# The two residual products of a two-layer block, cut by half of the features and 512 columns instead of by 256 columns

## The reference, cut to what matters

```python
# first layer: two mixed branches, back to the residual
x = x + jnp.einsum('bsd,de->bse', merged, w_out[layer])
# second layer: 16 learned meta tokens ahead of the 1024
h = jnp.concatenate([meta, x], axis=1)
u = rmsnorm(h, norm_mix_w);  proj = u @ w_in
h = h + jnp.concatenate([o_gla, o_swa], axis=-1) @ w_out
f = rmsnorm(h, norm_ff_w)
return h + jnp.square(jax.nn.relu(f @ w_ff1)) @ w_ff2
```

## Time and profile before

| | |
|---|---|
| median of 3 runs | 2725.63 us |
| profiled execution | 2722.03 us |
| its span (first to last instruction) | 2720.5 us |
| mean granted TensorE clock | 0.978 of full speed |
| VectorE, ScalarE, GpSimd busy | 61%, 40%, 8% |
| moved by DMA | 278.54 MB, 102 GB/s over the span |

### The profile page before, as it was taken

One profiled execution on the slowest core, in us unless ns is written; L12 is line 12 of the kernel. 1 busy time (PEld: TensorE's weight loads), 2 busy tenths in 40 slices (PEclk: granted clock), 3 DMA queues, 4 the chain that ended last, 5 costly groups with the idle time before them and its releaser, 6 DMA issues.

```text
span 2720.5 us, 33228 instructions
## 1 busy us (share of the span) xinstructions
PE 2594.9 (95%) x13064; PEld 2131.8 (78%) x13064; DVE 1648.4 (61%) x2130; ACT 1092.2 (40%) x1735; POOL 206.7 (8%) x351
## 2 busy tenths in 40 slices
PE   6999999999999999999999989998999999999998
PEld 5777888887776777878898766896798888878886
DVE  7665556555656564566534375156746767687779
ACT  6544222333656565124214143134425444443333
POOL 0001111110000001000111000000010212110000
PEclk9999999999999999999999989998999999999999
DMA  3222332333112113550333000110033444474432
GB/s 134 89 93 97 97 120 96 97 118 140 47 62 77 59 53 137 187 187 32 95 119 126 32 16 17 47 32 16 16 102 114 146 156 148 159 291 155 154 125 108
DMA packets 136098, 278.54 MB, mean 102 GB/s; under 512 B 8573, under 2 KB 93226, under 8 KB 128154
## 3 DMA queue, kind: packets, MB, share of 16 engines
q1 hardware_dynamic: 106026, 176.52, 19.1%
q0 software_dynamic: 29936, 100.14, 10.3%
HBM read 196.93 MB, written 79.69 MB: 102 GB/s over the span
## 4 chain that ended last, share of the span: by engine, by line
PE 80%; DVE 7%; ACT 4%; issue 3%; DVEq 2%; DMA 1%; ACTq 1%; POOL 0%; SPq 0%; POOLq 0%
PE ps L2423 31%; PE ps L506 12%; PE ps L2991 8%; PE ps L500 7%; PE ps L2517 3%; PE ps L2501 2%; PE ps L2871 2%; PE ps L2474 2%; PE ps L2800 1%; PE ps L2886 1%; PE ps L2680 1%; DVEq L1799 1%; PE ps L2431 1%; PE ps L2485 1%; PE ps L2652 1%
## 5 line engine op out<-in xcount | busy, mean ns | idle before, releaser
L1722 DVE TENSOR_TENSOR proj_out<-ps,proj_out 128x512 f32<-128x512 f32 x292 | 195.9, 686 | 264.4 <-PE ps L2423 259.4
L2423 PE MATMUL ps<-a_hi,pw_hi 128*128 128x512 f32 x528 | 215.9, 409 | 0.8 <-ACT proj_out L1112 0.8
L2423 PE MATMUL ps<-a_lo,pw_hi 128*128 128x512 f32 x528 | 209.9, 397 | 0.0
L2423 PE MATMUL ps<-t_hi,pw_hi 128*128 128x512 f32 x464 | 189.0, 407 | 0.0
L500 PE MATMUL ps<-w_hi,a_hi 128*128 128x256 f32 x640 | 181.7, 284 | 5.1 <-DVE a_lo L2129 5.1
L500 PE MATMUL ps<-w_lo,a_hi 128*128 128x256 f32 x640 | 181.3, 283 | 0.0
L500 PE MATMUL ps<-w_hi,a_lo 128*128 128x256 f32 x640 | 181.3, 283 | 0.0
L2423 PE MATMUL ps<-t_lo,pw_hi 128*128 128x512 f32 x464 | 180.9, 390 | 0.0
L485 DVE TENSOR_TENSOR w_lo<-w_raw,w_hi 128x2048 fp32r<-128x2048 f32 x28 | 64.1, 2289 | 132.4 <-ACT w_hi L481 132.4
L2423 PE MATMUL ps<-a_hi,pw_lo 128*128 128x512 f32 x352 | 138.4, 393 | 0.0
L481 ACT ACTIVATE w_hi<-w_raw 128x2048 fp32r<-128x2048 f32 x28 | 53.6, 1913 | 189.8 <-DMA w_raw<-in_w_out 85.8
(11 more groups left out here) (462 smaller groups left out, 6737.5 us busy)
## 6 DMA issues: line engine op xcount, KB each, us to landing
pw_raw<-in_w_in SPq DMA_DIRECT2D x30, 1024.0 KB, 5.6
hidden_raw<-hidden_forms SPq DMA_DIRECT2D x28, 1024.0 KB, 4.8
projections<-proj_out POOLq DMA_DIRECT2D x88, 256.0 KB, 3.4
w_raw<-in_w_in SPq DMA_DIRECT2D x20, 1024.0 KB, 5.1
pw_raw<-in_w_ff SPq DMA_DIRECT2D x16, 1024.0 KB, 6.2
w_quarter<-in_w_ff SPq DMA_DIRECT2D x16, 1024.0 KB, 7.2
hidden_forms<-proj_out POOLq DMA_DIRECT2D x56, 256.0 KB, 2.9
hidden_forms<-nb POOLq DMA_DIRECT2D x56, 256.0 KB, 3.4
```

Of the source, the lines that this page charges most:

```text
L1722: return dve.tensor_tensor(out_ap(n, j), product_bank(n, o), src, ALU.add)
L2423: last = pe.matmul(product_bank(n, o), w, a[:, k0 + k, t], start=(k == 0 and g == 0), stop=(k == 3 and g == 2))
```

## The change

- Each of the two products runs in four passes i = 0 to 3: the output columns c = i // 2 (512 of them) over the half i % 2 of the features (4 feature tiles). A pass goes through all 8 row tiles, each in a bank of its own, `row_bank(t) = (t + 4) % 8`, so 8 banks are open over two passes. A row tile takes 4 x 3 matmuls of 512 columns in a pass.
- In the first product the half with the tiles 0 to 3 goes first (`m_lo` 4), in the second the half with the tiles 4 to 7 (11 for row tiles 0 to 3, 14 for the others). The other halves wait for 8 and 10, or 13 and 16.
- A weight block is 4 feature tiles x 512 columns (`load_rows`, `half_rows`), again 1 MB.
- An add takes two banks and 512 columns of each. There are 8 adds to a product instead of 16, with residual loads of 512 KB into larger `XB` buffers.
- The low split of pass 2 moves between the adds of the first columns, and that of pass 3 behind them.
- The meta rows are turned after row tile 1 of pass 2, into bank 3. Turns 0 to 4 follow row tiles 3 to 7 of pass 3, one each. Turn 5 comes in the middle of the next block's output 0 (`halfway`), turns 6 and 7 after it.

The core of the diff:

```diff
+        def half_rows(w):
+            return w[:, :, :].rearrange("p a b -> p (a b)").rearrange("p (k c) -> p k c", c=HALF)
+        def row_bank(t):
+            return (t + 4) % 8
...
             def turn(self, pe, t):
                 pe.wait_ge(self.scaled, self.m + t + 1)
-                if self.m + t >= 1 and t != 1:
-                    pe.wait_ge(self.lo, self.m + t - (1 if t else 0))
+                if t >= 2:
+                    pe.wait_ge(self.lo, self.m + t - 1)
+                elif t == 1:
+                    pe.wait_ge(kept[1], kept_by(self.n))
...
+            def load_rows(n, s, src):
+                sp.wait_ge(gp_done, 4 * n + 4)
+                sp.dma_start(half_rows(W_raw[s]), src).then_inc(w_loaded[s], 16)
...
             def residual_blocks(B, again, norm, XB, next_weights, between=None):
-                for b in range(3):
-                    split_lo(dve, B + b + 1, (b + 1) % 2)
-                    for j in range(4):
-                        add(b, j)
-                        if between:
-                            between(b, j)
-                norm.dve(dve, lambda j: add(3, j), next_weights)
+                def add(c, j):
+                    dve.wait_ge(gp_done, done(B + 2 * c + 1, j))
+                    dve.wait_ge(xb_in[j % 2], again + 32 * c + 16 * (j // 2) + 16)
+                    b = row_bank(2 * j)
+                    dve.tensor_tensor(X1[:, 2 * j:2 * j + 2, c * HALF:(c + 1) * HALF], ps[:, b:b + 2, :], XB[j % 2][:, :, :],
+                                      ALU.add).then_inc(kept[j], 2)
+                split_lo(dve, B + 1, 1)
+                if between:
+                    between(0, 1)
+                    between(0, 3)
+                for j in range(4):
+                    add(0, j)
+                    if j == 1:
+                        split_lo(dve, B + 2, 0)
+                split_lo(dve, B + 3, 1)
+                if between:
+                    between(1, 3)
+                norm.dve(dve, lambda j: add(1, j), next_weights)
...
+            def residual_blocks(B, low, halves, parts, norm, bank_free):
+                for i in range(4):
+                    n, s = B + i, i % 2
+                    pe.wait_ge(w_lo, n + 1)
+                    for t in range(TT):
+                        if i < 2 and t % 4 == 0:
+                            pe.wait_ge(low, parts[i][t // 4])
+                        if i == 0:
+                            bank_free(t)
+                        if i == 2 and t % 2 == 0:
+                            pe.wait_ge(kept[t // 2], kept_by(B + 1))
+                        tok = slice(META + t * P, META + (t + 1) * P)
+                        for k in range(4):
+                            kk = 4 * halves[s] + k
+                            for g, (a, w) in enumerate(((A_hi, W_hi), (A_hi, W_lo), (A_lo, W_hi))):
+                                last = pe.matmul(bank[row_bank(t)], a[:, kk, tok], half_rows(w[s])[:, k, :],
+                                                 start=(s == 0 and k == 0 and g == 0), stop=(s == 1 and k == 3 and g == 2))
+                        if t % 2:
+                            last.then_inc(gp_done, 1)
+                        if i == 2 and t == 1 and norm.m:
+                            pe.wait_ge(kept[3], kept_by(B + 1))
+                            norm.turn(pe, -1)
+                        if i == 2 and t == 6 and norm.m:
+                            pe.wait_ge(norm.lo, norm.m)
+                        if i == 3 and t >= 3:
+                            norm.turn(pe, t - 3)
+            residual_blocks(L5, m_lo, (0, 1), ((4, 4), (8, 10)), n2, row_banks_free)
...
+            def mix_banks_free(t):
+                if t < 4:
+                    pe.wait_ge(gn_read, 4 + t + 1)
+                else:
+                    pe.wait_ge(kept[t - 4], kept_by(L7 - 1))
...
+            residual_blocks(L7, m_lo, (1, 0), ((11, 14), (13, 16)), n3, mix_banks_free)
```

More of the change, by code:

```diff
@@ L170, in build @@
     R_lo = at("ret_lo", [P, KT, SEQ], f32r, off=out_at)
-    pos[0] = work_at + 64 * 1024
-    XB = [work(f"xb{u}", [P, 2, BC]) for u in range(2)]
+    XB = [at(f"xb{u}", [P, 2, HALF], off=work_at + (56 + 4 * u) * KB) for u in range(2)]
     pos[0] = work_at
@@ L223, in build @@
     G3 = at("g3", [P, DM], off=region + 128 * KB)
-    XB7 = [at(f"xb7{u}", [P, 2, BC], off=region + (116 + 2 * u) * KB) for u in range(2)]
+    XB7 = [at(f"xb7{u}", [P, 2, HALF], off=region + (116, 100)[u] * KB) for u in range(2)]
     FD_hi = at("first_hidden_hi", [P, KT, BC], f32r, off=region + 106 * KB)
@@ L426, in turn, with last_turns @@
                 last.then_inc(self.turned, 1)
[L428 to L432, removed]
+            def last_turns(self, pe):
+                self.turn(pe, TT - 2)
+                self.turn(pe, TT - 1)
         class TokenSumNorm(LateNorm):
@@ L485, in split_lo, with gemm @@
             dve.tensor_tensor(W_lo[s][:, :, :], W_raw[s][:, :, :], W_hi[s][:, :, :].bitcast(f32), ALU.subtract).then_inc(w_lo, 1)
-        def gemm(pe, n, s, hi, lo, rows_out, between=None, before=None, banks=range(4), W_hi=W_hi, W_lo=W_lo):
+        def gemm(pe, n, s, hi, lo, rows_out, between=None, before=None, halfway=None, banks=range(4), W_hi=W_hi, W_lo=W_lo):
             pe.wait_ge(w_lo, n + 1)
@@ L837, in _ @@
             wo_d = w_out[0].rearrange("(k p) c -> p k c", p=P)
-            with sp.Fori(0, 2) as i:
+            def load_rows(n, s, src):
+                sp.wait_ge(gp_done, 4 * n + 4)
+                sp.dma_start(half_rows(W_raw[s]), src).then_inc(w_loaded[s], 16)
+            for c in range(2):
                 for s in range(2):
-                    load_block(sp, L5 + 2 * i + s, s, wo_d[:, :, ds(i * (2 * BC) + s * BC, BC)])
+                    load_rows(L5 + 2 * c + s, s, wo_d[:, 4 * s:4 * s + 4, c * HALF:(c + 1) * HALF])
             w6_d = w_in_2[0].rearrange("(k p) c -> p k c", p=P)
@@ L2657, in _ @@
                 gemm(pe, B2 + b, b % 2, S_hi, R_lo, False)
-            def residual_blocks(B, low, parts, norm, banks_free=None):
-                def operand_ready(j):
-                    if j % 2 == 0:
-                        pe.wait_ge(low, parts[j // 2])
-                    if banks_free:
-                        banks_free(j)
-                gemm(pe, B, 0, A_hi, A_lo, True, before=operand_ready)
-                gemm(pe, B + 1, 1, A_hi, A_lo, True)
-                gemm(pe, B + 2, 0, A_hi, A_lo, True)
-                if norm.m:
-                    norm.turn(pe, -1)
-                gemm(pe, B + 3, 1, A_hi, A_lo, True, between=lambda j: norm.pe_between(pe, j))
@@ L2715, in first_window_rows @@
                     rope_product(j - 1, NB[j - 1][:, :])
-            gemm(pe, L6, 0, A_hi, A_lo, False, between=first_window_rows, before=lambda j: after_norm(n2, j))
+            gemm(pe, L6, 0, A_hi, A_lo, False, between=first_window_rows, before=lambda j: after_norm(n2, j), halfway=lambda: n2.turn(pe, 5))
             gemm(pe, L6 + 1, 1, A_hi, A_lo, False, between=lambda j: rope_product(j + 3, NB[(j + 3) % 4][:, :]))
```

59 lines of the change are left out of this document (27 added, 32 removed).

## The result

The changed kernel takes 2730.7 us, the median of 20 runs (2726.94 to 2737.47), beside 2724.78 us for 20 runs of the kernel before (2721.08 to 2733.56). The ratio is 1.0018, interval 1.0009 to 1.0026: 5 us slower (5.9 by the medians). That is inside the forecast range (2716 to 2734) and within 0.5%, but the forecast was no change (-0.7 us), and the interval excludes no change. The profiled execution took 2732.57 us, its span is 2730.9 us and its granted clock 0.972 (before 2722.03, 2720.5, 0.978).

What follows compares the result with a forecast made beforehand. TensorE, busy for 95% of the span, was taken as the bound. First product +6.4 us and second -7.1 gave -0.7: 2721.3 us from the profiled 2722.03, or 2725 set against the median; range 2716 to 2734.

Steps and rivals of the forecast that it cites:

- Matmuls: Both products: 512-column matmuls at 231.4 ns make each pass 0.52 us shorter, 2.1 us less a product.
- Start of the second product: Second product follows the last gate matmul at once: 5.1 us of waiting and 2.4 of slow start go, -7.5.
- Rival 4: Second product still can't start, its banks, low parts or weights being late: +6.8, 2732 us; chance 0.10.
- Meta rows: First product, turn of 16 meta rows: 5.6 us wait, 2.4 slow clock, less the old wait: net +6.0 us.
- rival 2: First product's meta wait is cheaper, clock staying at 2.4 GHz, load quick: +3.0 for +6.0, 2722 us; chance 0.17.
- Adds and the closing chain: End of each product: four adds, +0.53 us each, lengthen the VectorE and ScalarE chain; +2.0 us a product.
- my walk: Turn-by-turn estimate of TensorE's closing waits; in the second product about 1.0, 2.8, 2.3, 1.0, 1.7 and 1.7 us.
- rival 3: Closing chains fall to the lower clock, three spells of 2.4 us: 2737 us, half of it 2731; chance 0.15.
- Sum of the own parts: Terms of both products added: first product +6.4 us, second -7.1, together -0.7 us.
- The bound I set: Whole kernel: a change of over 10 us either way means something acts that is not in the sum.

Runs made afterwards that it cites:

- e1: New first product with the old second product, against the kernel before: 2738.55 us, ratio 1.0045.
- e2: New second product with the old first product, against the kernel before: 2720.88 us, ratio 0.9982.
- e3: Changed kernel with the meta rows turned after row tile 5 of pass 2 instead of 1: 2728.82 us, 1.0005 against the kernel before.
- e4: Kernel before with 12 overwritten matmuls of 256 columns added ahead of the first product: 2727.27 us, ratio 1.0006.
- e5: Kernel before with 22 overwritten matmuls of 256 columns added ahead of the first product: 2726.02 us, ratio 1.0006.
- e6: e3's kernel with 6 overwritten matmuls of 512 columns added ahead of the first product: 2728.89 us, 1.0001 against the kernel before.
- e7: e3's kernel with 11 overwritten matmuls of 512 columns added ahead of the first product: 2727.95 us, 1.0002 against the kernel before.
- e10: e3's kernel with 46 unused dense matmuls in TensorE's waits from rope product to gates: 2725.26 us, 0.9980 against the kernel before.
- e12: Kernel before with 24 gate matmuls moved ahead of level 1 of the second half, then 4 a level: 2740.91 us, ratio 1.0058.
- e14: Changed kernel with 3 unused dense matmuls in each second-half level 1 to 7, 12 in the 5 us wait: 2729.73 us, 1.0018 against the kernel before.
- e15: Kernel before with 3 unused dense matmuls in each second-half level 1 to 7 and 12 in the 5 us wait: 2728.54 us, ratio 1.0016.

## Why the prediction was right, and where it was wrong

*Matmuls.* Right: 231.7 ns where 231.4 was taken, in both products.

*Start of the second product.* Right: no gap and a clock of 1.00. e1, with the old form, still has the 5.1 us wait; e2 doesn't. Rival 4 is out.

*Meta rows.* Right in cause and nearly in size: 5.04 us of waiting for 5.6, close to the lower end of 5.0. From issue to ScalarE it took 5.02 us, where 5.4 was taken. The slow clock behind it came (0.53 from 1436 to 1439 us) and cost 1.7 us in the next 96 matmuls (23.98 us for 22.24) and 0.3 in the turn (1.00 for 0.66), where 2.4 was taken; rival 2 had it stay at 1.00. e3 confirms the price by taking the term away: the wait and the slow spell were forecast at 5.6 + 2.4 = 8.0 us, and its rest is 7.0 us less than that of after (2265.4 for 2272.4).

*Adds and the closing chain.* Right: an add takes 1.22 us, and the cycles are 8.03 us (1468.39 to 1476.42) and 9.48 (2066.66 to 2076.14), which is 7.49 + 0.53 and 8.94 + 0.53 to 0.01 us. The waits of the second tail (7.8 us) are longer than before (5.6) and shorter than my walk had them (10.5), and the projections come when forecast, counted from the last gate matmul (128.8 us for 135.7). Each tail has one short spell at the lower clock (0.66 from 1476 to 1481 us and from 2083 to 2088), with a cycle of 8.28 instead of 8.03 us in the first; rival 3's three spells with 7.2 us lost didn't appear.

*Sum of the own parts.* Both products and all that lies outside the stage: -1.3 us in the profiles, -0.7 forecast. By product: +5.9 at the rope product (+6.4 forecast) and -6.95 (-7.1 forecast).

*The step that failed* isn't among the parts: it is the unwritten one that everything between the products would shift as a block, a term put at nothing without a reason. It measured +11.7 us in the pair of profiles and 5 to 6 us in the means, through the granted clock of two stages where TensorE's work is partly waits or short matmuls. It could have been read beforehand: the trace of the kernel before has its second half at 0.82, and the three runs shown spread over 12 us. I priced the clock only where the change touched a wait. The bound I set, 10 us for something "which is not in the sum", was met by the profiled pair (+10.4 us of span), but not by the medians (+5.9). And 0.5% was too coarse for what a measurement can tell: with 20 runs a side the interval is 0.17% wide.

**What stays open.** Why the new first product lowers the clock so much later. Shown: it is that product (e1 and e2), not its meta wait (e3), and not lateness of the stretch (e3 is early; e4 and e5 are late in the old kernel). Suggested only: small shifts move the clock of the new kernel (e6, e7). Not tried: which part of the new first product does it. The half passes, the adds over two banks, the larger residual loads and the single turns were always changed together. The chain from the end of that product to the attention's timing wasn't found.

**What beats both.** The second product alone (e2): 2720.88 us, 0.9982 (0.9965 to 0.9999). It keeps the -5.6 us and leaves the first product as it was. e10, the late meta turn with filled waits, has 0.9980 (0.9962 to 0.9999). Both intervals only just exclude no change, and they are the best of sixteen experiments, so some of it may be luck.

## What to carry to other kernels

A sum of the parts that an edit touches is only half of a forecast: list also the later stages whose granted clock lies between its two levels, since the same instructions there may take some 10% more or less after an edit ahead of them, or from one run to the next (121.1 and 112.3 us for the attention, 83.7 and 74.5 for the second half in e3 and e7), and put that spread into the range and the chances. Compare kernels at the same mean clock as well as by the median, and two edits by their own stretches, before a loss of 0.2% is laid on what was edited. When an edit moves two places with opposite signs, run each alone: here the second product's half gave 5 us and the first product's cost 12.

## What the runs showed of the hardware that was not expected

- TensorE's clock stays at its lower level (0.50) for 36.6 us without an idle gap in the trace (e12), while it runs 32 short matmuls and 4 dense ones in turn. With 7 dense ones such levels were seen at 0.50 (after, up to 1937.1 us) and at 1.00 (before, from 1910.1 us); with 10 (e14, e15) at 0.85 and 0.93 over the half.
- The same 402 matmuls of the second half took 74.5 us at a clock of 0.84 (e7) and 83.7 at 0.73 (e3): 12% for one stage, 0.3% of the kernel.
- The same wait of 5 us in the second half goes with a spell of 13.7 us at the lower clock in some profiles (before, e7) and of 30.7 in others (after, e3).
- Dense filler in waits, 46 matmuls that no result needs, cost the changed kernel nothing net: 0.9998 (0.9982 to 1.0013) with them, 1.0018 without, since its clock rose from 0.9729 to 0.9789. The kernel before lost 0.2% by them (1.0019, from 1.0001 to 1.0037), with its clock nearly unchanged.
